# Cross attention's scores and weighings as three fp32r passes over high and low halves

## The reference, cut to what matters

```
q = (rmsnorm(x) @ w_cq);  k, v = split(rmsnorm(mem) @ w_ckv)
sc = einsum('bshd,bmhd->bhsm', q, k) * 256 ** -0.5
p = softmax(sc, axis=-1);  o = einsum('bhsm,bmhd->bshd', p, v)
x = x + o @ w_co
```

## Time and profile before

| | us |
|---|---|
| median of 3 runs | 1585.64 |
| lowest, highest | 1585.33, 1586.15 |
| span of the profiled execution | 1583.6 |
| median less span | 2.0 |

### The profile page before, as it was taken

How to read it: one execution, slowest core, us unless ns; L and a number is a source line. 1 busy time by engine, 2 the same in 40 slices (tenths; PEclk the granted TensorE clock), 3 DMA queues, 4 the chain that set the end, 5 groups by cost and what they waited for, 6 DMA issues and landing times.

```text
span 1583.6 us, 19738 instructions
## 1 busy us (share of the span) xinstructions
PE 1565.6 (99%) x7812; PEld 1255.7 (79%) x7812; DVE 851.5 (54%) x1288; ACT 604.6 (38%) x967; POOL 643.7 (41%) x289
## 2 busy tenths in 40 slices
PE   8999999999999999999999999999999999999998
PEld 6877767788887788777887788888888888888887
DVE  3447685675224556552235755477687772534425
ACT  5624444664333532223222344653234332222223
POOL 3533323355831434443443343344235444444441
PEclk9999999999999999999999999999999999999999
DMA  5532121243541268872333234221243233333331
GB/s 168 173 94 67 58 63 54 82 131 95 172 134 40 81 199 283 274 252 85 107 101 107 83 103 141 75 67 55 67 146 107 84 102 93 94 105 95 94 98 62
DMA packets 268990, 177.75 MB, mean 112 GB/s; under 512 B 8329, under 2 KB 247083, under 8 KB 268644
## 3 DMA queue, kind: packets, MB, share of 16 engines
q1 hardware_dynamic: 254860, 147.20, 31.3%
q10 hardware_dynamic: 13480, 27.18, 4.9%
q0 software_dynamic: 560, 2.12, 0.4%
HBM read 171.72 MB, written 4.76 MB: 111 GB/s over the span
## 4 chain that ended last, share of the span: by engine, by line
PE 95%; DVE 2%; ACT 2%; issue 1%; DMA 0%; SPq 0%; ACTq 0%; DVEq 0%
PE ps L1220 57%; PE ps L1232 12%; PE ps L1246 7%; PE ps L1381 3%; PE ps L1395 2%; PE ps L1386 2%; PE ps L1556 1%; PE ps L1537 1%; PE ps L1451 1%; PE ps L1437 1%; PE ps L1315 1%; PE ps L1474 1%; PE ps L1423 1%; PE ps L1460 1%; PE ps L1623 0%
## 5 line engine op out<-in xcount | busy, mean ns | idle before, releaser
L631 POOL TENSOR_TENSOR WL<-raw,WH 128x1024 fp32r<-128x1024 f32 (+2 forms) x272 | 629.5, 2316 | 914.4 <-ACT WH L668 914.2
L668 ACT ACTIVATE WH<-raw 128x1024 fp32r<-128x1024 f32 (+2 forms) x272 | 275.9, 1015 | 729.9 <-PE ps L1220 542.3
L1220 PE MATMUL ps<-hH,WH 128*128 128x512 f32 x688 | 171.5, 391 | 0.0
L1220 PE MATMUL ps<-hL,WH 128*128 128x512 f32 x688 | 170.0, 389 | 0.0
L1220 PE MATMUL ps<-hH,WL 128*128 128x512 f32 x688 | 169.9, 389 | 0.0
L1220 PEld LDWEIGHTS ps<-hH,WH 128*128 128x128 f32 x688 | 128.2, 188 | 30.2 <-issue 4.0
L1220 PEld LDWEIGHTS ps<-hL,WH 128*128 128x128 f32 x688 | 129.1, 188 | 26.9
L1220 PEld LDWEIGHTS ps<-hH,WL 128*128 128x128 f32 x688 | 129.1, 188 | 26.8
L1232 PE MATMUL ps<-hH,WH 128*128 128x512 f32 x288 | 118.9, 413 | 0.1
L1232 PE MATMUL ps<-hH,WL 128*128 128x512 f32 x288 | 113.0, 392 | 0.0
L1232 PE MATMUL ps<-hL,WH 128*128 128x512 f32 x288 | 112.5, 391 | 0.0
(11 more groups left out here) (563 smaller groups left out, 2727.1 us busy)
## 6 DMA issues: line engine op xcount, KB each, us to landing
raw<-in_w_in_dram SPq DMA_DIRECT2D x64, 512.0 KB, 3.7
raw<-in_w_mlp_dram SPq DMA_DIRECT2D x64, 512.0 KB, 3.9
raw<-in_w_gate_up_dram SPq DMA_DIRECT2D x44, 512.0 KB, 3.8
ada_w<-in_w_ada_dram ACTq DMA_DIRECT2D x40, 512.0 KB, 5.2
raw<-in_w_out_dram SPq DMA_DIRECT2D x16, 512.0 KB, 4.0
raw<-in_w_ckv_dram SPq DMA_DIRECT2D x16, 512.0 KB, 3.8
raw<-in_w_down_dram SPq DMA_DIRECT2D x16, 448.0 KB, 3.8
raw<-in_w_cq_dram SPq DMA_DIRECT2D x8, 512.0 KB, 4.6
```

The lines of the kernel that those rows point to most:

```text
L631: pool.tensor_tensor(WL[un.slot][:, 0:s_.kt, 0:n], raw[un.slot][:, 0:s_.kt, 0:n], WH[un.slot][:, 0:s_.kt, 0:n].bitcast(F32), ALU.subtract) ...
L668: act.activation(WH[un.slot][:, 0:s_.kt, 0:n], raw[un.slot][:, 0:s_.kt, 0:n], ACT.Copy).then_inc(high_done, 1)
L1220: ins = pe.matmul(dst, w[un.slot][:, q, 0:m], a[:, q, :], start=(k == 0), stop=(k == 3 * kt - 1))
```

## The change

Keys, values, queries and turned probabilities are each kept as a high and a low half in fp32r, and score and weighing become three passes. Who makes the halves:

- Keys: VectorE multiplies by rm inside PSUM, ACT copies the high half (`key_high`), VectorE subtracts (`key_tile`). Values: ACT scales into the high half, VectorE makes the low one. Both follow `high(u + 3)` of the same unit in ACT's order.
- Queries: they aren't multiplied by r. ACT copies the high half (`query_high`) after `high(u + 3)` for the first three units and before it in the steps; VectorE subtracts (`query_tile`), and only then is the bank given back.
- Turned probabilities: ACT copies the high half (and raises `turn_high`), VectorE subtracts in the next step, ahead of its maximum (`turn_low`), and this raises `kept`. Turn m is thus kept in VectorE's step m + 3.
- r: PE sums the squares to a column for each block of 128 tokens (`token_sums`, eight calls of one column), VectorE and ACT work on 128 x 4, and the exponential takes r/16 as its scale.

Some semaphores are merged so that there are enough of them, in the same order of loads and waits; those lines and the unchanged layout are left out.

```diff
@@ -211,13 +212,17 @@
         memH = z("memH", 40, [P, DT, MEM], F32R)
         memL = z("memL", 64, [P, DT, MEM], F32R)
         rm = z("rm", 88, [P, MEM])
-        kc = z("kc", 48, [P, DT, MEM])
-        vc = z("vc", 56, [P, 2, D])
-        qc = z("qc", 64, [P, DT, S])
+        kcH = z("kcH", 48, [P, DT, MEM], F32R)
+        kcL = z("kcL", 96, [P, DT, MEM], F32R)
+        vcH = z("vcH", 56, [P, 2, D], F32R)
+        vcL = z("vcL", 80, [P, 2, D], F32R)
+        qcH = z("qcH", 64, [P, DT // 2, S], F32R)
+        qcL = z("qcL", 72, [P, DT // 2, S], F32R)
         oH = z("oH", 0, [P, DT, S], F32R)
         oL = z("oL", 16, [P, DT, S], F32R)
         pC = [z(f"pC{i}", 32 + i, [P, MEM]) for i in range(4)]
-        pcT = [z(f"pcT{i}", 36 + 4 * i, [P, 2, S]) for i in range(2)]
+        pcH = [z(f"pcH{i}", 36 + 4 * i, [P, 2, S], F32R) for i in range(2)]
+        pcL = [place(f"pcL{i}", [P, 2, S], F32R, at=tmp_at + 4096 * i) for i in range(2)]
 
         fH = z("fH", 0, [P, FT, S], F32R)
         fL = z("fL", 44, [P, FT, S], F32R)
...
@@ -861,19 +870,43 @@
                     side_keep("mem", rm)
                 squared(un, g="norm_cross_g")
             follow("out", crossed)
+            def key_high(un):
+                act.wait_ge(key_ok, un.i + 1)
+                act.activation(kcH[:, un.i, :], bank(un.bank, MEM), ACT.Copy).then_inc(cross_high, 1)
+
+            def value_high(un):
+
+                if un.i % 4 < 3:
+                    return
+                for tt, b in enumerate(at["mv", un.i - 1 + n].bank for n in range(2)):
+                    if tt == 0:
+                        act.wait_ge(v_done, 9 + un.i // 4 + 1)
+                    act.activation(vcH[:, tt, un.i // 4 * S:(un.i // 4 + 1) * S], bank(b), ACT.Identity,
+                                   scale=tok_r[:, 8 + tt:9 + tt]).then_inc(cross_high, 1)
+
+            def query_high(un):
+                if un.i >= 4:
+
+                    act.wait_ge(scored["c"], 4 * (un.i // 2 - 1))
+                act.wait_ge(unit_done, un.u + 1)
+                act.activation(qcH[:, un.i % 4, :], bank(un.bank), ACT.Copy).then_inc(cross_high, 1)
+
             for i in range(SLOTS):
                 high(at["mk", i].u + SLOTS)
-            stat("cross", r)
-            follow("mk", lo=SLOTS)
-            follow("mv")
+                key_high(at["mk", i])
+            root_table()
+            act.wait_ge(stat_v, stat_no["cross"] + 1)
+            act.activation(tok_r[:, 0:4], tok_r[:, 0:4], ACT.Sqrt, scale=1.0 / 256).then_inc(stat_r, 1)
+            follow("mk", key_high, lo=SLOTS)
+            follow("mv", value_high)
 
             def exp_c(n):
                 act.wait_ge(maxed["c"], n + 1)
                 if n >= 4:
                     act.wait_ge(turned["c"], n - 3)
                 k = 2 * (n % 4)
-                act.activation(pC[n % 4][:], bank(3 + n % 3, MEM), ACT.Exp, bias=tiny[:, k:k + 1], scale=1.0 / 16,
-                               accum_out=tiny[:, 8 + k:9 + k]).then_inc(exped["c"], 1)
+                act.activation(pC[n % 4][:], bank(3 + n % 3, MEM), ACT.Exp, bias=tiny[:, k:k + 1],
+                               scale=tok_r[:, n % ST:n % ST + 1], accum_out=tiny[:, 8 + k:9 + k]).then_inc(exped["c"], 1)
 
             def keep_c(m):
                 h, qt = m // ST, m % ST
...
@@ -881,8 +914,8 @@
                 if h >= 2:
 
                     act.wait_ge(pv_done["c"], h - 1)
-                act.activation(pcT[h % 2][:, :, qt * P:(qt + 1) * P],
-                               bank(7, MEM).rearrange("p (t c) -> p t c", c=P), ACT.Copy).then_inc(kept["c"], 1)
+                act.activation(pcH[h % 2][:, :, qt * P:(qt + 1) * P],
+                               bank(7, MEM).rearrange("p (t c) -> p t c", c=P), ACT.Copy).then_inc(turn_high, 1)
 
             def high_c(h):
                 act.wait_ge(pv_done["c"], h + 1)
...
@@ -892,10 +925,13 @@
 
             for i in range(3):
                 high(at["cq", i].u + SLOTS)
+                query_high(at["cq", i])
+            act.wait_ge(stat_r, stat_no["cross"] + 1)
             for s_ in range(C_ITEMS + 2):
                 if s_ < C_ITEMS:
                     exp_c(s_)
                 for un in cross_ended(s_):
+                    query_high(un)
                     high(un.u + SLOTS)
                 if s_ >= 2:
                     keep_c(s_ - 2)
...
@@ -1522,7 +1558,10 @@
             spread(6, 8, 2).then_inc(stat_sum, 1)
             units("out", mgH, mgL, S, 1)
             units("mk", memH, memL, MEM, 0, 3)
-            stat("out")
+            pe.wait_ge(res["out"], DT)
+            token_sums(acc, 0)
+            pe.wait_ge(res_sq["out"], DT)
+            token_sums(tmp[1], 4).then_inc(stat_sum, 1)
             units("mk", memH, memL, MEM, 3)
             for lo in (0, 4):
                 values("mv", tokens("mv", (memH, memL), 2, lo), lo)
...
@@ -1534,8 +1573,10 @@
                 if n % ST == 0:
                     pe.wait_ge(bank_free, at["cq", 2 * h + 1].out + 1)
                 for j in range(2):
-                    ins = pe.matmul(bank(3 + n % 3, MEM), qc[:, 2 * h + j, q], kc[:, 2 * h + j, :],
-                                    start=(j == 0), stop=(j == 1))
+                    k, at_q = 2 * h + j, (2 * h + j) % 4
+                    for e, (a, b) in enumerate(((qcH, kcH), (qcH, kcL), (qcL, kcH))):
+                        ins = pe.matmul(bank(3 + n % 3, MEM), a[:, at_q, q], b[:, k, :],
+                                        start=(j == 0 and e == 0), stop=(j == 1 and e == 2))
                 ins.then_inc(scored["c"], 1)
 
             def turn_c(m):
...
@@ -1553,7 +1594,9 @@
                 for j, b_ in enumerate((2, 6)):
                     c = slice((2 * h + j) * P, (2 * h + j + 1) * P)
                     for b in range(2):
-                        ins = pe.matmul(bank(b_), vc[:, b, c], pcT[h % 2][:, b, :], start=(b == 0), stop=(b == 1))
+                        for e, (v, p) in enumerate(((vcH, pcH), (vcH, pcL), (vcL, pcH))):
+                            ins = pe.matmul(bank(b_), v[:, b, c], p[h % 2][:, b, :], start=(b == 0 and e == 0),
+                                            stop=(b == 1 and e == 2))
                 ins.then_inc(pv_done["c"], 1)
 
             for i in range(3):
...
@@ -2286,21 +2329,42 @@
             dve.wait_ge(stat_r, stat_no["mem"] + 1)
 
 
-            one = times_r(lambda i: kc[:, i, :], rm, MEM)
-            each("mk", one, 0, 3)
-            stat("cross")
-            each("mk", one, 3)
+            def key_tile(un):
+                b = bank(un.bank, MEM)
+                dve.wait_ge(unit_done, un.u + 1)
+                dve.tensor_tensor(b, b, rm[:], ALU.mult).then_inc(key_ok, 1)
+                dve.wait_ge(cross_high, KEY_HIGH + un.i + 1)
+                rest(b, kcH[:, un.i, :], kcL[:, un.i, :]).then_inc(bank_free, 1)
+                taken(un)
+
+            def query_tile(un):
+                dve.wait_ge(cross_high, QUERY_HIGH + un.i + 1)
+                rest(bank(un.bank), qcH[:, un.i % 4, :], qcL[:, un.i % 4, :]).then_inc(bank_free, 1)
+
+            def value_low(e, tt):
+                some = slice(e * S, (e + 1) * S)
+                dve.wait_ge(cross_high, VALUE_HIGH + 2 * e + tt + 1)
+                low(bank(at["mv", 4 * e + 2 + tt].bank), tok_r[:, 8 + tt:9 + tt], vcH[:, tt, some],
+                    vcL[:, tt, some]).then_inc(bank_free, 1)
+
+            each("mk", key_tile, 0, 3)
+            dve.wait_ge(stat_sum, stat_no["cross"] + 1)
+            own.step(dve.tensor_scalar(tok_r[:, 0:4], ps[:, 7, 0:4], 1.0 / D, EPS, ALU.mult, ALU.add))
+            own.step(dve.scalar_tensor_tensor(tok_r[:, 0:4], ps[:, 7, 4:8], 1.0 / D, tok_r[:, 0:4], ALU.mult, ALU.add))
+            dve.reciprocal(tok_r[:, 0:4], tok_r[:, 0:4]).then_inc(stat_v, 1)
+            each("mk", key_tile, 3)
+            dve.wait_ge(stat_r, stat_no["cross"] + 1)
+            own.step(dve.tensor_scalar(tok_r[:, 4:8], tok_r[:, 0:4], -1.0, None, ALU.mult))
             for e in range(2):
-                values("mv", 9 + e, [(vc[:, tt, e * S:(e + 1) * S], None, tok_r[:, 8 + tt:9 + tt], True) for tt in range(2)], 4 * e)
-            dve.wait_ge(stat_r, stat_no["cross"] + 1)
-
-            query_tile = times_r(lambda i: qc[:, i, :])
+                for tt in range(2):
+                    value_low(e, tt)
 
             def max_c(n):
                 k = 2 * (n % 4)
                 dve.wait_ge(scored["c"], n + 1)
                 own.step(dve.tensor_reduce(tiny[:, k:k + 1], bank(3 + n % 3, MEM), AX.X, ALU.max))
-                dve.tensor_scalar(tiny[:, k:k + 1], tiny[:, k:k + 1], -1.0 / 16, None, ALU.mult).then_inc(maxed["c"], 1)
+                dve.tensor_scalar(tiny[:, k:k + 1], tiny[:, k:k + 1], tok_r[:, 4 + n % ST:5 + n % ST], None,
+                                  ALU.mult).then_inc(maxed["c"], 1)
 
             def norm_c(n):
                 k, p = 2 * (n % 4), pC[n % 4][:]
...
@@ -2316,13 +2380,21 @@
```

(39 more changed lines are left out.)

4 lines of the change are left out of this document (2 added, 2 removed).

## The result

| | before | after |
|---|---|---|
| median, us | 1585.64 | 1592.09 |
| executions timed | 1585.1 to 1586.15 | 1592.39, 1592.00, 1592.57, 1588.47, 1592.09 |
| span of the profiled execution, us | 1583.6 | 1590.5 |

The account below looks back on a forecast made before the run. TensorE, busy for 99% of the span, was taken to bound the kernel. The terms -5.1 + 0.1 + 3.1 + 0.2 + 7.4 = +5.7 us gave 1591.3 us, range 1584.5 to 1596.

Parts of the forecast that it names:

- scores and weighings: TensorE's own work: sixteen scores save 2.2 us and four weighings 2.9 us as fp32r passes, together 5.1 us.
- sums for r: TensorE's sums of squares: sixteen one-column instructions take 1.92 us instead of 1.72, 0.1 us more (bounds 0 and 0.2).
- `cq`, with restart: Third query projection unit: TensorE waits 3.1 us for query tile 0's subtraction behind a late slab, plus 0.2 us restart.
- turns, with restarts: Five turns wait for VectorE's subtraction: 8.1 us less the 0.7 lost now, 7.4 us (6 to 8.5).
- about even: Rival: slab comes nearly in time, two of five turns covered by slack; +0 to +1 us, 1586.0 us, chance 0.16.
- The rival that the fp32r passes aren't cheaper: Three fp32r passes cost as much as plain fp32, so the 5.1 us saving is gone; 1596.4 us, chance 0.08.
- Copies of keys and values cost nothing: Key tiles' added copy and subtraction (0.37 and 0.42 us) are covered, a bank being needed again 2.9 us later.
- the slab lands at 446.0: Weight slab of `cq` 3, queued behind the context load, leaves 2.7 us later and lands at 446.0 instead of 443.29.
- The bound of 0.4 and the bound of 3.9: TensorE's wait at `cq` 2: 0.4 us if the slab landed at 443.29, 3.9 if delayed fully with crowded loads.
- All five: Uncovered turn hand-overs in steps 9, 11, 13, 15, 17: losses 1.5, 1.9, 1.5, 1.0 and 2.2 us.
- the clock falls in the wait of `cq` 2: Rival: TensorE drops to 1.2 GHz there, half the unit's matmuls costing 2.7 us more; 1594.0 us, chance 0.17.
- the faster rival: Turn hand-overs stay covered, only today's 0.7 us is lost, and the slab lands as now; 1581.0 us, chance 0.12.

Follow-up runs that it names:

- the filled turn: Changed kernel with eight spare 128x512 matmuls in step 17, ahead of the turn that waits 2.0 us; 1588.94 us, ratio 1.002.
- steps without low halves: Changed kernel without the low half of the turned probabilities, the second weighing pass using the high half again; 1584.73 us, ratio 0.9991.
- query first: Changed kernel with ScalarE making the high half of query tiles 0 to 2 ahead of the next slab's high half; 1588.81 us, ratio 1.0019.
- the mended order: Changed kernel with query copies ahead of the slab, PSUM copies ahead of slab rounding, turn subtractions earlier and head outputs later; 1581.61 us, ratio 0.9977.

## Why the prediction was right, and where it wasn't

I forecast 1591.3 us, slower by 5.7; it is 1592.09, slower by 6.5. The direction and the cause hold. The size is partly luck: two costs were too large and two falls of the clock, which I hadn't in the sum, filled the gap. Without the falls the change would cost 3.1 us less, by the filled turn, so slower by some 3 us and not by 5.7.

| term, us | predicted | measured | by what |
|---|---|---|---|
| scores and weighings | -5.1 | -4.7 | steps without low halves |
| sums for r | +0.1 | +0.06 | ledger |
| `cq`, with restart | +3.3 | +1.7 | ledger; gone in two kernels |
| turns, with restarts | +7.4 | +6.2 | 74.8 - 73.3 + 4.7 |
| clock at 519 us | 0 | +1.5 | 76.3 against 74.8 |
| clock at 949 us | 0 | +1.6 | 219.3 against 217.6 |
| start, ahead of the change | 0 | +0.5 | ledger |
| sum, of the span | +5.7 | +6.9 | |

The last term is a difference between two executions in the first 304 us; other kernels of the study begin at 302.9 to 304.3, the changed part being the same. It isn't the change's. Two slips of the prediction's own sums: its upper bounds add up to +7.7 and not +7.5, and its "about even" rival, -5.1 + 0.1 + 0.4 + 0.2 + 7.4 less 3 to 4, gives -1 to 0 and not 0 to +1. Neither bears on the forecast.

- **TensorE's own work.** Right in kind and nearly in size: scores take 0.71 us for 0.72, weighings 2.77 for 2.72. The rival that the fp32r passes aren't cheaper is refuted.
- **Copies of keys and values cost nothing.** Right: 38.0 us for that stage, and no wait in it.
- **The wait at `cq`.** The mechanism is as told, down to each link: ScalarE idle before the slab, then slab, copy, subtraction, TensorE. The size failed at one step, "the slab lands at 446.0". This execution runs 0.5 us late from its start, so I count from the first matmul of `cq` (434.39 before, 434.94 after). The context's load left 2.7 us later than before (at 438.59), just as I had it. The slab landed 6.4 us behind it instead of 7.9, at 444.97, and so only 1.1 us later than before where I had 2.7. That is 1.6 of the 1.7 us by which the wait was over-sized. The timelines of ScalarE and of SyncE's queue, then the window from the issue of the context's load to the slab's landing, before and after:

```profile
444.97 1.06 ACT L677 ACTIVATE WH<-raw 128x1024 fp32r<-128x1024 f32 x1 [7.27 <-DMA raw<-in_w_cq_dram]
445.93 0.58 ACT L892 ACTIVATE qcH<-ps 128x512 fp32r<-128x512 f32 x1
```

```profile
438.59 0.37 SPq L606 DMA_DIRECT2D ctxtok<-in_ctx_dram  x1
```

```profile
435.37:443.29 7.92, 7.92 (x37) 6.56 (x36) 0.69 (x1) 1.06 (x1) 3.23 (x2) 1.00 0.93 281
```

```profile
438.59:444.97 6.38, 6.38 (x30) 5.29 (x29) 0.00 (x0) 0.00 (x1) 0.44 (x1) 1.00 0.88 273
```

I chose "3.1, because the queue is served in order and its rate is taken up". The rate was nearly the same, 281 and 273 GB/s, and in both kernels the loads ahead had stopped moving when the context's was issued (1 GB/s at 435.0 to 435.37 before, 0 at 437.0 to 438.6 here). But 2.22 MB moved in the first window and 1.74 MB in the second, for 1.5 MB of context and slab. So in the kernel before more of the loads queued behind the slab was moved before its last piece landed; why more there, no run shows. The bound of 0.4 and the bound of 3.9 held the wait; my choice between them was too near the upper end. The ScalarE copy also started 0.1 us before the slab's rounding was listed as ended, which the sum of lengths doesn't show.
- **The steps.** All five were named, and no other turn waits. Idle time predicted (the loss less its restart) against measured: step 9 1.3 and 1.23, step 11 1.7 and 1.59, step 13 1.3 and 1.30, step 15 0.8 and 0.56, step 17 2.0 and 2.01. What was over-sized is the restart. I added 0.2 us to each wait, 1.0 in all. The stage shows 74.8 - 73.3 + 4.7 = 6.2 us, and the idle time is 6.7 less the 0.5 of before, so 6.2: nothing measurable is left for restarts. The other kernels bear that out. The steps less their idle time are 68.1 us with five waits (query first), 68.0 with four (71.5 - 3.5), 68.2 with four small ones (69.6 - 1.4) and 68.1 with one. A turn that runs 0.41 us after a wait overlaps the matmuls behind it, and I counted that overlap as cost.
- **The clock.** Here the prediction failed. Its rival had the right mechanism at the wrong place: "the clock falls in the wait of `cq` 2". No fall came there; the wait was 1.4 us. It came behind the wait of step 17, which my own list gave as the longest of the steps, and behind tiny matmuls 430 us later. I had tied the rival to the one wait that I took for the longest and priced it at 2.7 us; each fall cost 1.5 to 1.6. By the Trainium skill, "TensorE: Matmul & The Clock Gate", section "What's actually happening", the chip looks at activity in a window that runs free of the kernel, so that the moment of a change depends on where the work falls in it. The table of waits above agrees in that the same gap of 2.0 us was followed by a fall in three traces and not in two. By that rule it would also differ between executions of one kernel; no run here shows it, since no kernel with this wait has a second trace.
- **The even and the faster rival.** The turns weren't covered by slack; VectorE's idle time did lie ahead of the semaphore. But the time of 1581.0 that the faster rival gives is nearly what the mended order reaches, 1581.6: its condition could nearly be made true by moving a few calls (1.4 us of idle time is left in the steps).

Open: whether the fifth execution of the changed kernel, at 1588.5 us, had neither fall; 3.6 us is somewhat more than the price of two, and it has no trace. What besides the wait decides a fall is open too. Nor was it tried to bring step 11 and step 15 under cover, where 1.0 us is left.

## What to carry to other kernels

When a step gains a second half (copy, then subtract), price the hand-over, not the work: count from the event that frees the copy to the semaphore that the bottleneck engine waits for, and put the subtraction and the copy at the front of each engine's list for the step. Here the order of a few calls was worth 10.5 us (1592.1 against 1581.6), more than twice what the cheaper matmuls save: 1.7 at `cq`, 5.2 in the steps, and about 3 in two falls of the clock that came with the waits. If a copy that the bottleneck waits for is queued behind a copy that waits for a load, either swap them or load earlier; either is worth the whole wait. And compare stage by stage at one clock: a difference of 1.6 us far from the change can be the clock of TensorE, and filling a wait with spare matmuls shows it.

## What the runs showed of the hardware

- One wait of 2.0 us, in a stretch that has four others of 0.6 to 1.6 us, was followed by a fall of TensorE's clock to 1.2 GHz; the fall began about 0.8 us after work had resumed (518.7 against 517.85) and lasted some 3.4 us. With the wait filled it did not come, and neither in two traces with the same wait 1.4 and 1.8 us earlier. The price was 1.5 to 1.6 us each time it was seen (76.3 against 74.8, 219.3 against 217.6, 43.1 against 41.5).
- An engine listed as busy can lose its clock: sixteen matmuls of one column (1.92 us) or of 8x8 (1.95 us) were followed by a fall, without any idle time that would explain it, in some kernels and not in others with the same instructions.
- Spare matmuls can shorten a program: eight of them, 1.8 us of work in a wait of 2.0 us, took the time from 1592.1 to 1588.9 us.
- A wait of 0.3 to 2.0 us ahead of the transposes cost TensorE its idle time and no more: the steps less their idle time are 68.0 to 68.2 us with one wait or with five, though the first transposes behind a wait are listed with 0.41 us instead of 0.22. Ahead of the 512-column matmuls at `cq` a wait of 1.4 us cost 1.7.
- A slab's load that was issued, with the 1 MB load ahead of it, 2.7 us later against TensorE's work landed only 1.1 us later (444.97 - 434.94 against 443.29 - 434.39): at nearly the same rate 1.74 MB instead of 2.22 MB moved from the first issue to its landing.
